# Twenty small table loads moved from SyncE's DMA queue to GpSimd's in a two-layer decoder kernel

## What is computed

```python
for l in range(DEPTH):                       # DEPTH = 2
    h = rms_norm(x, norm_mix[l])
    if l % 2 == 0:
        mix = retention_hgrn2_mixer(h, w_in_ab[j], w_out_ab[j], ret_gnorm[j], lb_table[l], hgrn_onorm[j], cos_r, sin_r)
    else:
        mix = stickbreak_diff_mixer(h, w_in_cd[j], w_out_cd[j], diff_qnorm[j], diff_knorm[j], ..., diff_subln[j], cos_d, sin_d, l)
    x = x + mix
    h = rms_norm(x, norm_ffn[l])
    x = x + hierarchical_moe(h, router_group_w[l], router_group_b[l], router_expert_w[l], router_expert_b[l], w_gate[l], w_up[l], w_down[l])
```

## Time and profile before

| | us |
|---|---|
| median of 3 runs | 1401.58 |
| lowest and highest run | 1400.58, 1402.24 |
| profiled execution, span from first to last instruction | 1400.7 |
| TensorE busy in the span | 1296.7 |
| VectorE, ScalarE, GpSimd busy | 284.9, 201.1, 12.6 |

### The profile page before, as it was taken

One profiled execution on the slowest core, in us unless ns is written; L12 is line 12 of the kernel. 1 busy time (PEld: TensorE's weight loads), 2 busy tenths in 40 slices (PEclk: granted clock), 3 DMA queues, 4 the chain that ended last, 5 costly groups with the idle time before them and its releaser, 6 DMA issues.

```text
span 1400.7 us, 14604 instructions
## 1 busy us (share of the span) xinstructions
PE 1296.7 (93%) x5884; PEld 647.6 (46%) x5884; DVE 284.9 (20%) x700; ACT 201.1 (14%) x400; POOL 12.6 (1%) x12
## 2 busy tenths in 40 slices
PE   6999999999999999999969988899999999999997
PEld 5567544434444444444437444544444444454442
DVE  3310314111111111111130652411111111111111
ACT  3324111010010010101020131110010110001000
POOL 0000000000000000000000000100000000000000
PEclk9988999999999999999989998999999999999999
DMA  7952164799999999999993322487999999999992
GB/s 247 324 193 107 60 241 157 291 393 415 402 416 416 416 416 414 406 412 417 400 353 120 120 82 95 184 348 299 415 418 414 401 416 416 415 417 414 416 401 112
DMA packets 55695, 448.19 MB, mean 320 GB/s; under 512 B 13040, under 2 KB 13296, under 8 KB 30960
## 3 DMA queue, kind: packets, MB, share of 16 engines
q1 hardware_dynamic: 55664, 447.74, 79.1%
HBM read 446.68 MB, written 1.05 MB: 320 GB/s over the span
## 4 chain that ended last, share of the span: by engine, by line
PE 87%; issue 3%; ACT 3%; DVE 3%; SPq 3%; DMA 1%; DVEq 0%; ACTq 0%
PE psum L468 30%; PE psum L491 15%; PE psum L688 10%; PE psum L435 9%; PE psum L428 9%; PE psum L731 4%; PE psum L683 2%; SPq L334 2%; PE psum L470 1%; ACT mixed L523 1%; PE psum L784 1%; PE psum L493 1%; PE psum L417 1%; PE psum L786 1%; ACT arena L524 1%
## 5 line engine op out<-in xcount | busy, mean ns | idle before, releaser
L468 PE MATMUL psum<-ring,mixed 128*64 128x512 f32 x992 | 437.5, 594 | 2.3 <-issue 2.3
L470 PE MATMUL psum<-ring,mixed 128*64 128x512 f32 x992 | 437.6, 594 | 0.0
L491 PE MATMUL psum<-ring,mixed 128*64 128x512 f32 x512 | 225.8, 594 | 43.2 <-ACT arena L524 43.2
L468 PEld LDWEIGHTS psum<-ring,mixed 128*64 128x64 f32 x992 | 133.1, 137 | 277.8 <-issue 277.8
L493 PE MATMUL psum<-ring,mixed 128*64 128x512 f32 x512 | 226.6, 595 | 0.0
L688 PE MATMUL psum<-ring,hT 128*128 128x512 f32 x320 | 146.4, 616 | 3.3 <-DMA ring<-in_w_in_ab 3.3
L491 PEld LDWEIGHTS psum<-ring,mixed 128*64 128x64 f32 x512 | 67.5, 137 | 167.3 <-issue 159.1
L470 PEld LDWEIGHTS psum<-ring,mixed 128*64 128x64 f32 x992 | 133.1, 137 | 0.0
L428 PEld LDWEIGHTS psum<-arena,h 128*128 128x128 f32 x1032 | 117.8, 192 | 28.3 <-issue 26.0
L435 PE MATMUL psum<-arena 128*128 128x512 f32 x272 | 125.8, 605 | 1.6 <-DVE arena L574 1.6
L428 PE MATMUL psum<-arena,h 128*128 128x128 f32 x1032 | 124.2, 278 | 2.1 <-DVE arena L542 2.1
(11 more groups left out here) (246 smaller groups left out, 709.3 us busy)
## 6 DMA issues: line engine op xcount, KB each, us to landing
ring<-in_w_up SPq DMA_DIRECT2D x64, 2048.0 KB, 10.9
ring<-in_w_down SPq DMA_DIRECT2D x64, 2048.0 KB, 9.0
ring<-in_w_gate SPq DMA_DIRECT2D x60, 2048.0 KB, 11.6
ring<-in_w_in_ab SPq DMA_DIRECT2D x8, 2048.0 KB, 16.5
ring<-in_w_in_cd SPq DMA_DIRECT2D x6, 2048.0 KB, 16.7
arena<-in_w_gate SPq DMA_DIRECT2D x4, 2048.0 KB, 14.5
ring<-in_w_out_ab SPq DMA_DIRECT2D x2, 2048.0 KB, 13.0
ring<-in_w_out_cd SPq DMA_DIRECT2D x2, 2048.0 KB, 7.3
```

The lines of the kernel that those rows point to most:

```text
L468: pe.matmul(psum[0:SLOTS, bank, :], xT[:, c, 0:SLOTS], wa[:, c, :], start=c == 0, stop=c == KC - 1)
L470: mm = pe.matmul(psum[SLOTS:P, bank, :], xT[:, c, SLOTS:P], wb[:, c, :], start=c == 0, stop=c == KC - 1)
L491: pe.matmul(psum[0:SLOTS, YB + n, :], actT[:, c, 0:SLOTS], wa[:, c, 512 * n:512 * (n + 1)], start=c == 0, stop=c == FC - 1)
```

## The change

The loop over `small_loads` is taken out of SP's block and put at the head of GpSimd's block. The destinations, the sources, the order and the semaphore are the same; only the issuing engine differs.

```diff
--- before.py
+++ after.py
@@ -312,27 +312,6 @@
                 sp.dma_start(pos_i[:, :], t["positions"].rearrange("b (c p) -> p (b c)", p=P)).then_inc(S["pos_landed"], 16)
                 sp.dma_start(lbt[:, :, :], t["hgrn_lb_logits"].rearrange("r (h p) -> p r h", p=P)).then_inc(S["lb_landed"], 16)
                 load_in(0, 1)
-                small_loads = [
-                    (consts[:, FIRST_CONSTS:], t["consts"][:, FIRST_CONSTS:]),
-                    (retg[:, 0, :], t["ret_gnorm"].rearrange("a h d -> a (h d)").broadcast_to([P, GROUP_W])),
-                    (retg[:, 1, :], t["hgrn_onorm"].rearrange("a h d -> a (h d)").broadcast_to([P, GROUP_W])),
-                    (dg[:, 0, :], t["diff_qnorm"].broadcast_to([P, 64])),
-                    (dg[:, 1, :], t["diff_knorm"].broadcast_to([P, 64])),
-                    (dlam[:, 0, :], t["diff_lam_q1"].broadcast_to([P, 64])),
-                    (dlam[:, 1, :], t["diff_lam_k1"].broadcast_to([P, 64])),
-                    (dlam[:, 2, :], t["diff_lam_q2"].broadcast_to([P, 64])),
-                    (dlam[:, 3, :], t["diff_lam_k2"].broadcast_to([P, 64])),
-                    (subln[:, :], t["diff_subln"].broadcast_to([P, HD])),
-                ]
-                for l in range(2):
-                    small_loads.append((gcol[:, l, :], t["norm_ffn"][l].rearrange("(c p) -> p c", p=P)))
-                    small_loads.append((rw[:, l, :, 0:4], t["router_group_w"][l].rearrange("(c p) n -> p c n", p=P)))
-                    small_loads.append((rw[:, l, :, 4:36], t["router_expert_w"][l].rearrange("(c p) n -> p c n", p=P)))
-                    small_loads.append((rb[:, l, 0:4], t["router_group_b"][l:l + 1, :].broadcast_to([P, 4])))
-                    small_loads.append((rb[:, l, 4:36], t["router_expert_b"][l:l + 1, :].broadcast_to([P, 32])))
-                for dst, src in small_loads:
-                    sp.dma_start(dst, src).then_inc(S["small_landed"], 16)
-            assert len(small_loads) == N_SMALL
 
             for layer in range(2):
                 base = unit_base(layer)
@@ -1110,6 +1089,28 @@
 
         @block.gpsimd
         def _(pool):
+            with nc.allow_non_contiguous_dma("small tables"):
+                small_loads = [
+                    (consts[:, FIRST_CONSTS:], t["consts"][:, FIRST_CONSTS:]),
+                    (retg[:, 0, :], t["ret_gnorm"].rearrange("a h d -> a (h d)").broadcast_to([P, GROUP_W])),
+                    (retg[:, 1, :], t["hgrn_onorm"].rearrange("a h d -> a (h d)").broadcast_to([P, GROUP_W])),
+                    (dg[:, 0, :], t["diff_qnorm"].broadcast_to([P, 64])),
+                    (dg[:, 1, :], t["diff_knorm"].broadcast_to([P, 64])),
+                    (dlam[:, 0, :], t["diff_lam_q1"].broadcast_to([P, 64])),
+                    (dlam[:, 1, :], t["diff_lam_k1"].broadcast_to([P, 64])),
+                    (dlam[:, 2, :], t["diff_lam_q2"].broadcast_to([P, 64])),
+                    (dlam[:, 3, :], t["diff_lam_k2"].broadcast_to([P, 64])),
+                    (subln[:, :], t["diff_subln"].broadcast_to([P, HD])),
+                ]
+                for l in range(2):
+                    small_loads.append((gcol[:, l, :], t["norm_ffn"][l].rearrange("(c p) -> p c", p=P)))
+                    small_loads.append((rw[:, l, :, 0:4], t["router_group_w"][l].rearrange("(c p) n -> p c n", p=P)))
+                    small_loads.append((rw[:, l, :, 4:36], t["router_expert_w"][l].rearrange("(c p) n -> p c n", p=P)))
+                    small_loads.append((rb[:, l, 0:4], t["router_group_b"][l:l + 1, :].broadcast_to([P, 4])))
+                    small_loads.append((rb[:, l, 4:36], t["router_expert_b"][l:l + 1, :].broadcast_to([P, 32])))
+                for dst, src in small_loads:
+                    pool.dma_start(dst, src).then_inc(S["small_landed"], 16)
+            assert len(small_loads) == N_SMALL
             pool.wait_ge(S["h_turned"], 1)
             nc.gpsimd.memset(ke0, 0.0)
             nc.gpsimd.memset(ke1, 0.0).then_inc(S["zeroed"], 1)
```

## The result

The change makes the kernel slower: 1415.46 us (median of four runs, 1413.12 to 1417.30) against 1401.91 us (four runs, 1400.58 to 1402.82), a ratio of 1.0103 with a 95% interval from 1.0088 to 1.0117. That is 13.6 us, and outside the range I gave. The profiled execution spans 1414.7 us, 14.0 more than that of the kernel before, and took 1416.65 us by its own time.

A forecast was written before the change was run, and what follows sets the result against it. TensorE was taken to bound the kernel, 87% of the span. The terms -3.35 - 1.93 + 3.9 + 1.0 + 0 summed to -0.4 us, forecasting 1401.2 us, no change; the range went from 1398.3 to 1411 us.

The forecast's parts named there:

- The stall and its clock: TensorE at unit 2: its wait for weights goes, -3.35 us, and the low clock behind it, -1.93 us.
- What the start pays: bytes in front of unit 0: First projection: ten GpSimd loads, 2.67 MB, delay unit 0, so TensorE starts +3.9 us later; bounds +2.0 and +6.5.
- The clock at the start: First projection: a longer idle gap ahead of it may lower TensorE's clock; between 0 and +1.93 us, taken as +1.0.
- The tables' due time: VectorE's wait for all twenty tables: they land at about 45 us, free up to 55.1 us; term 0.
- rival 1: Wait ahead of line 1326: tables land too late and hold back `project(0, 3)`; some 1409.5 us, or 1411; chance 14%.
- Rival 2: GpSimd's DMA issues progress only while VectorE is idle, so tables land at 59.2 us; 1405.3 us; chance 8%.
- Rival 3: Start: tables get in front of `x` and gain; start +6.5 and a cold clock, 1404.8 us; chance 5%.
- Rivals 4: Start is spared: only `consts` delays unit 0 and the clock holds; -3.3 us, 1398.3 us; chance 13%.
- Rival 5: Unit 2 is late all the same, as short pieces clog the DMA engines; 1405 us; chance 2%.
- A rule set aside: Skill rule that another issuing engine saves only small issue time; by it unit 2 gains nothing, leaving the start's +3.9.

The follow-up runs named there:

- the late start on GpSimd's queue: Against the kernel before, GpSimd issues all twenty tables but first waits until unit 1 has landed: 1397.56 us, ratio 0.9965.
- the constants alone: Against the kernel before, GpSimd issues only the rest of `consts`, SyncE keeps the other nineteen tables: 1401.13 us, ratio 0.9999.

## Why the prediction was wrong, point by point

**The stall and its clock, right.** Forecast -3.35 and -1.93 us, measured -3.35 and -1.96. Unit 2 lands in time, and from 63.81 us the 64 matmuls run in 27.47 us (forecast 27.5).

**"What the start pays: bytes in front of unit 0", the step that failed.** The place was right, unit 0 on the shared engines, and the runs that vary only this place bear it out: the late start on GpSimd's queue brings the loss to nothing. The size was wrong, +3.9 us forecast, +16.8 measured, and beyond my bound of +6.5. I priced ten tables by their bytes, "2608 KB = 2.67 MB, or 6.5 us at 408 GB/s". Two things are in that price.

- Of the tables only the constants go by bytes: 4.6 us by 408 GB/s, 4.8 us of engines. The other nineteen cost 10.1 us of engines for 1.13 MB, of which some 4.6 us is that partitions read the same row (14.6 with, 10.0 without).
- I left the other ten tables out, without a reason. As unit 0 is held back it meets them all. It lands at 31.8 us, and GpSimd had issued its last table at 14.2.

"If the two queues share the engines evenly" was right in packets, and no help, since the packets are unequal.

The rows that could have told were there, in the kernel before. From 25 to 34 us the DMAs moved 36 GB/s at a share of 0.21: engine time that is 0.21 x 9 = 1.9 us for 0.32 MB, where 408 GB/s would need 0.8. I read it as SyncE being slow to issue short pieces, and priced the DMAs themselves by the full rate. The row of SyncE's queue for 34 to 41 us has the rest of the small tables:

```profile
q1 hardware_dynamic: 5609, 0.35, 57.9%
```

That is 0.579 x 7 = 4.1 us for 0.35 MB. With these 6.0 us for the small ones, and the constants and `retg` by their bytes (2.41 MB, 5.9 us), the twenty would have been 11.9 us of engines, an estimate, against 14.6 measured and 6.5 in my sum.

**The clock at the start.** +1.0 forecast, within 0 to 1.93; measured +2.66, after an idle 15.28 us at the end of which the granted clock is 0.50. Mis-sized; the low granted clock follows from the late unit 0, but not surely the whole 2.66 us (last section).

**The tables' due time, right in its sum.** Term 0, measured 0: line 1327 is released by ScalarE. My 45 us was far too late: the last issue ends at 14.2 us, and the 0.9 us for a table in short pieces lies even below SyncE's 1.49. The 7.66 us in my upper bound was, as rival 1 itself suspected, an issue into a queue with work ahead in it.

**The rivals.** Rival 1 (tables too late) fell with that. Rival 2 (VectorE holds GpSimd up) isn't seen: GpSimd's issues follow at 0.53 to 0.9 us with no pause, but the test is weak. Only the last three issues overlap line 602 on VectorE, from 12.33 to 14.2 us, and in the run with the late start, where they take the same 0.54 to 0.90 us, VectorE is busy 1.46 of the 14 us. Rival 3 (GpSimd's packets take more than half of the engines) named the mechanism, with 5%, and its own sum stopped at +6.5 for want of the price of a packet; my mark for it, a start "past 23 us", is what came. The gain was late by 4.0 us, `x` not at all (ScalarE's squares begin at 5.76 us). Rivals 4 and 5 didn't come: unit 0 wasn't spared, and unit 2 wasn't late. Rival 5's argument, "2 us of engine work at most" in the short pieces, was wrong even so: its row ends at 34 us, and 4.1 us more come behind it.

**A rule set aside.** The Trainium skill's "Issuing engines are not separate DMA queues" (page "DMA: Bandwidth & Descriptors") has the queues interleave on the same engines and only issue time to be saved. The first half carried more than I let it: it was cited for what issue time is worth, and the loss came by the interleaving; here the trace agrees, with the 84 to 82 packets above. On the second half the trace keeps its own number, -5.3 us for an earlier issue of unit 2.

**What stays open.** Unit 0 is late by up to 3.2 us more than q0's engine time (17.8 against 14.6). A packet of SyncE's holds an engine 0.107 us from 10 to 12 us (0.275 x 32 / 82), where in the kernel before it was 0.088 in the same stretch (382 packets at a share of 1.045); for the 64 packets of 2 KB that each engine has of unit 0 that is some 1.2 us, an estimate. The rest stays open. Nor is it shown why the tables, read from different rows, still take 10.0 - 7.4 = 2.6 us more than by bytes. Most of it, 2.9 - 0.7 = 2.2 us, goes with the six of short pieces, yet reading them contiguously saved only 0.6 (14.6 to 14.0). And that one row is dear is shown by a change of source alone; what in the memory or the engines makes it so isn't.

## What to carry to other kernels

A second DMA queue is not a free lane: here the load that the first matmul waits for shared each engine packet by packet with whatever the other queue had, and waited for nearly all of it. Price a table by the engine time that its packets took in a trace (share times window), best of the same issuing engine, not by its bytes, above all where all partitions read one row. If an order on one queue is the problem, change that order first: unit 2 ahead of the tables, one line, gives 0.35%, and moving the tables to GpSimd's queue gives the same only if they wait until the first units have landed.

## What the hardware showed that I had not expected

**A table of one row for all partitions.** The same 880 packets and 3.01 MB take 14.6 us of sixteen engines when thirteen tables read one row each, 10.0 us when they read 128.

**Pieces and packets.** On GpSimd's queue the six tables of short pieces, 6144 pieces, take at most 224 packets. On SyncE's queue, in the kernel before from 34 to 41 us, 5599 of 5609 packets are under 512 bytes.

**Half pace at a full granted clock.** The 128 matmuls of units 0 and 1 took 27.89 us in the profiles of the kernel before and of the one with unit 2 first, and 29.68, 29.94 and 30.90 us in three others whose start lies within 0.3 us of these. TensorE's windows with the late tables (us, PE busy with its matmuls, granted clock, DMA share, GB/s):

```profile
20.00:22.00 2.00, 2.00 (x6) 1.00 1.05 386
22.00:24.00 2.00, 2.00 (x8) 1.00 1.05 387
24.00:26.00 2.00, 2.00 (x11) 1.00 1.06 433
```

Six matmuls in 2 us in place of eleven, the pace that the changed kernel has at a granted 0.50, and the row says 1.00. TensorE had been idle for 1.41 us ahead of them, as in the kernel before, where eleven run from the start. The run with the positions' wait moved has the same after a longer gap: TensorE idle for 14.2 us, six matmuls from 34 to 36 us, and again the row says 1.00. So the row can miss a slow stretch; what slows it there is not shown. All six runs with over 8 us of idle time ahead of the projections took 29.47 to 30.63 us for the 128 matmuls. So up to 3.0 us of a single profile hang on this, and two profiles of such kernels can't be compared to better than that; medians of several runs suffer less. It also means that the +2.66 of the account above, and the +1.84 with the constants alone, are sizes that could have come by themselves, and I can't say how much of them is due to the change.
